# Two attentions of a two-block transformer kernel: scores as keys by tokens, less maxima found ahead of them

## The chip, the cores and the metric

The kernel runs on one core of one Trainium2 chip. It is one program for five engines: PE (TensorE, the matrix engine), DVE (VectorE), ACT (ScalarE), POOL (GpSimd) and SP (SyncE, which here only issues the transfers). The metric is the time of one launch in microseconds (us) on the device, lower is better; the figure compared is the median over runs. The trace comes from one more execution, which was profiled.

## The reference

Four sub-layers are added to a residual x of 256 tokens by 1024, all in float32: an NSA attention, a MoBA attention, a feed-forward, a mixer of two attentions (MLA and FoX), and a second feed-forward. The change is in the first two. With 256 tokens, NSA's selection takes every block and its window every earlier token, and MoBA has one block, so their scores are plain causal ones:

```
# NSA: three branches for each of 16 query heads (4 key heads), head size 64
s_cmp = q @ k_cmp.T * scale      # 15 compressed keys a head
s_slc = q @ ks.T * scale         # keys of branch 1, causal mask
s_win = q @ kw.T * scale         # keys of branch 2, causal mask
o = gc[..., 0:1] * o_cmp + gc[..., 1:2] * o_slc + gc[..., 2:3] * o_win
y = (o * silu(z)) @ w_out        # o_x = softmax(s_x) @ v_x
# MoBA: one causal branch
p = softmax(q @ k.T * scale + causal); y = ((p @ v) * silu(z)) @ w_out
# both: h = rms_norm(x) * (1 + scale) + shift;  x = x + gate * y, where
shift, scale, gate = split(silu(c) @ ada_w[i] + ada_b[i], 3)
```

## The kernel before

**Weights.** All weights are one list of units of 128 x 1024 floats (512 KB), fetched in order by SP into a ring of 7 buffers (`raw`, NRAW = 7). A buffer is fetched again when its unit has been used. For a projection, ACT rounds a unit to `w_hi` (`rounds`, L888, fp32r, up to 3 units ahead), DVE forms the rest `w_lo` (`rests`, L1313), and PE multiplies three times, hi by hi, hi by lo, lo by hi (`linear`): with tokens as output rows 512 columns at a time (L451, 12 matmuls a unit), or with tokens as columns 256 at a time (L460, 24 matmuls a unit). Matmuls on these rounded values are fp32r; the others (scores, values, transposes) are full fp32.

**Adaptive weights.** `ada_w` has 12 chunks of 512 columns, four units each. Chunks 0 to 3 are multiplied by cond and summed by DVE (`mac_chunk`, L1408). Of 4 to 11, ACT scales each half unit in place (`scale_chunk`) and POOL adds it to an accumulator (`sum_chunk`, L1952). PE then sums a chunk over partitions (`ada_columns`: L486, or L488 for the gate chunks).

**The order** is written out by hand for each engine, as a list of calls, and `hook(i, step)` puts pieces of other work between the items of an attention. For NSA it is: projection z0 (4 units), two matmul groups of compressed scores, then `attention` over 32 items, one for each head and branch; the four units of z1 sit in its first items; then out0 and out1 (8 units), the norm of the next sub-layer, and MoBA's projections. MoBA's attention has 16 items.

**An item of `attention`** goes through all engines. PE scores tokens by keys (L588, L589) in full fp32; DVE adds the causal mask and finds each row's maximum (L1484, L1486), and scales it (L1494); ACT takes exp with the maximum as bias and sums the row (L1007); DVE takes the reciprocal (L1491), multiplies by the gate (L1502) and divides (L1504, L1505); PE transposes the three 128 x 128 blocks (L475); ACT copies them back (`prob_t`); PE multiplies by the values (L610, L612; L609 for the compressed branch) into `o_acc`, 64 rows for each head. Scores are five items ahead of values. At every pair's end DVE multiplies by the gate z (L1470), ACT rounds (o_hi), DVE forms o_lo (L1509).

**Between sub-layers** (`norm_turns`, L504) x is multiplied by a diagonal matrix of the norm's factors while it is transposed; so PE waits for squares, mean, power (POOL) and the diagonal (L1336). After MoBA and after the mixer x is instead transposed as it is (`plain_turns`) and the factor is applied later.

## Time and profile before

| | |
|---|---|
| median of 3 runs | 1008.74 us (1004.24 to 1011.91) |
| the profiled execution | 1017.86 us, of which its span is 1016.0 |
| PE busy | 941.6 us, 93% of the span |
| DVE, ACT, POOL busy | 601.0, 515.5, 173.2 us |
| longest groups | L1313 DVE w_lo, 300.8 us; L888 ACT w_hi, 259.2 us |
| PE, full fp32 scores | L588 and L589: 33.9 and 43.7 us |
| PE, values | L609, L610, L612: 13.6, 47.3, 28.1 us (all attentions) |
| mean granted clock of PE | 0.952 |
| weights moved | 163.28 MB, at 161 GB/s |

A time here is the time an instruction stood in its engine; matmuls overlap, so the pace of PE is best read from the chain, which gives a run of matmuls with its length and their number. Each MATMUL of full fp32 shows as two instructions. "PEclk" is the granted clock in tenths, or as a share, of 2.4 GHz: 0.50 is 1.2 GHz.

### The profile page before, as it was taken

The numbers are of one execution on the slowest core, as the hardware profiler recorded it, in microseconds if no ns is written. First come the engines' busy times: TensorE is split into PE (matmuls) and PEld (weight loads), VectorE is DVE, ScalarE is ACT, GpSimd is POOL, SyncE is SP. The second block draws the span as 40 slices with busy tenths as digits, with TensorE's granted clock in tenths as the row PEclk, the third lists the DMA queues.
The fourth block names the chain that finished last, engine by engine and source line by source line (L and its number), as shares of the span: only waits on it lengthen the run. The fifth ranks groups of instructions, "written<-read, shape, count | busy, mean of one in ns | idle before, by whom it ended". The sixth has DMA issues, their size and how long they took to land.

```text
span 1016.0 us, 13211 instructions
## 1 busy us (share of the span) xinstructions
PE 941.6 (93%) x4823; PEld 763.2 (75%) x4823; DVE 601.0 (59%) x1192; ACT 515.5 (51%) x940; POOL 173.2 (17%) x190
## 2 busy tenths in 40 slices
PE   2689988998989988999999998999899899999997
PEld 2578976555568964788888887889788788888886
DVE  4873567766457577675555444659345765555542
ACT  2233556765434476564444443667555464444431
POOL 0015424652002651010000000426000200000000
PEclk9889999767699998999999999999999999999999
DMA  9855725444055453356555653645233555565651
GB/s 344 307 153 179 248 75 178 144 145 125 0 166 165 147 172 98 107 175 201 181 181 177 208 171 110 197 145 157 77 120 105 166 166 186 185 201 174 201 152 41
DMA packets 45391, 163.28 MB, mean 161 GB/s; under 512 B 5136, under 2 KB 5392, under 8 KB 45328
## 3 DMA queue, kind: packets, MB, share of 16 engines
q1 hardware_dynamic: 45328, 162.44, 50.0%
q8 instruction: 39, 0.64, 0.3%
q14 instruction: 24, 0.20, 0.1%
HBM read 161.37 MB, written 1.05 MB: 160 GB/s over the span
## 4 chain that ended last, share of the span: by engine, by line
PE 85%; DVE 8%; ACT 3%; issue 2%; DMA 1%; SPq 0%; POOL 0%; DVEq 0%; ACTq 0%
PE bank L451 55%; PE bank L460 11%; PE bank L475 5%; PE bank L610 3%; PE bank L589 2%; PE bank L588 2%; PE bank L504 2%; PE bank L547 1%; PE bank L612 1%; DVE w_lo L1313 1%; DVE ada_acc L1408 1%; PE bank L609 1%; DMA w_raw<-in_weights 1%; DVE stats L1494 1%; ACT soft L1007 1%
## 5 line engine op out<-in xcount | busy, mean ns | idle before, releaser
L888 ACT ACTIVATE w_hi<-w_raw 128x1024 fp32r<-128x1024 f32 (+2 forms) x249 | 259.2, 1047 | 203.0 <-PE bank L451 174.5
L1313 DVE TENSOR_TENSOR w_lo<-w_raw,w_hi 128x1024 fp32r<-128x1024 f32 (+2 forms) x249 | 300.8, 1224 | 101.3 <-ACT w_hi L888 101.3
L451 PE MATMUL bank<-w_hi,h_hi 128*128 128x512 f32 (+1 forms) x576 | 229.4, 398 | 15.6 <-DVE w_lo L1313 8.2
L451 PE MATMUL bank<-w_hi,h_lo 128*128 128x512 f32 (+1 forms) x576 | 225.4, 391 | 0.0
L451 PE MATMUL bank<-w_lo,h_hi 128*128 128x512 f32 (+1 forms) x576 | 224.9, 390 | 0.0
L451 PEld LDWEIGHTS bank<-w_hi,h_hi 128*128 128x128 f32 x576 | 109.5, 190 | 37.4 <-issue 16.5
L451 PEld LDWEIGHTS bank<-w_hi,h_lo 128*128 128x128 f32 x576 | 109.2, 190 | 22.9
L451 PEld LDWEIGHTS bank<-w_lo,h_hi 128*128 128x128 f32 x576 | 109.7, 190 | 20.9
L1952 POOL TENSOR_TENSOR ada_acc<-ada_acc,w_raw 128x512 f32<-128x512 f32 x56 | 73.4, 1311 | 84.0 <-ACT w_raw L892 79.4
L460 PE MATMUL bank<-h_hi,w_hi 128*128 128x256 f32 x264 | 77.9, 295 | 0.2 <-ACT tok_k L892 0.2
L460 PE MATMUL bank<-h_lo,w_hi 128*128 128x256 f32 x264 | 75.2, 285 | 0.0
L460 PE MATMUL bank<-h_hi,w_lo 128*128 128x256 f32 x264 | 75.1, 284 | 0.0
L451 PE MATMUL bank<-w_hi,a_hi 128*128 128x512 f32 x176 | 70.3, 400 | 0.0
L451 PE MATMUL bank<-w_hi,a_lo 128*128 128x512 f32 x176 | 69.3, 394 | 0.0
L451 PE MATMUL bank<-w_lo,a_hi 128*128 128x512 f32 x176 | 69.1, 392 | 0.0
L1007 ACT ACTIVATE soft<-soft,stats 128x128 f32<-128x128 f32 (+1 forms) x128 | 56.7, 445 | 12.6 <-DVE stats L1494 12.6
L892 ACT ACTIVATE prob_t<-bank 128x384 f32<-128x384 f32 x64 | 31.1, 487 | 62.9 <-PE bank L475 62.7
L1762 DVE SCALAR_TENSOR_TENSOR act<-bank,stats,act 128x256 f32<-128x256 f32 x44 | 21.1, 483 | 67.2 <-ACT act L1187 67.2
L460 PEld LDWEIGHTS bank<-h_hi,w_hi 128*128 128x128 f32 x264 | 51.1, 194 | 2.3 <-issue 1.8
L460 PEld LDWEIGHTS bank<-h_lo,w_hi 128*128 128x128 f32 x264 | 51.2, 194 | 0.2
L460 PEld LDWEIGHTS bank<-h_hi,w_lo 128*128 128x128 f32 x264 | 51.0, 193 | 0.0
L589 PE MATMUL bank<-k_t,q_t 64*128 64x256 f32 (+2 forms) x128 | 43.7, 431 | 0.0
(258 smaller groups left out, 1412.6 us busy)
## 6 DMA issues: line engine op xcount, KB each, us to landing
w_raw<-in_weights SPq DMA_DIRECT2D x298, 512.0 KB, 4.0
w_raw<-in_weights SPq DMA_DIRECT2D x4, 360.0 KB, 3.1
x<-in_x SPq DMA_DIRECT2D x1, 1024.0 KB, 7.0
gate_bias<-in_gate_bias SPq DMA_DIRECT2D x2, 512.0 KB, 9.4
out<-x SPq DMA_DIRECT2D x1, 1024.0 KB, 4.0
w_raw<-in_weights SPq DMA_DIRECT2D x3, 256.0 KB, 2.7
const<-in_constants SPq DMA_DIRECT2D x1, 413.5 KB, 7.7
cols<-in_columns SPq DMA_DIRECT2D x1, 208.5 KB, 2.5
```

The lines of the kernel that those rows point to most:

```text
L451: mm = e.matmul(pb[t][:, 0:n], xs[q], ws[p], start=(k + kk == 0 and i == 0), stop=(k + kk == kts - 1 and i == 2))
L460: mm = e.matmul(o, ws[p], xs[q], start=(k + kk == 0 and i == 0 and b % 2 == 0), stop=(k + kk == kts - 1 and i == 2 and (b % 2 == 1 or b == ...
L475: mm = e.transpose(bank[0:int(np.prod(src.shape[1:])), o:o + src.shape[0]], src, ident)
L504: mm = e.matmul(b[:, o:o + P], x[:, t, (2 * kp + kk) * P:(2 * kp + kk + 1) * P], diag[:, t, :], start=True, stop=True)
L589: e.matmul(bank[:, P:3 * P], it["q"](1), it["k"](S), start=True, stop=True).then_inc(*scored((s, i)))
L610: e.matmul(o, it["v"](0), p[:, 0:S], start=it["first"] and not it["cmp"], stop=False, skip_group_check=True)
L888: e.activation(w_hi[i % NSPLIT][:, 0:c], raw[v % NRAW][:, 0:c], ACT.Copy).then_inc(*rounded(v))
L892: return e.activation(out, src, ACT.Copy, **more)
L1007: e.activation(m[:, c0:c1], m[:, c0:c1], ACT.Exp, bias=ng[:, t:t + 1], scale=it["scale"], accum_out=su[:, t:t + 1]).then_inc(*exped((s, j, ...
L1313: e.tensor_tensor(w_lo[i % NSPLIT][:, 0:c], raw[v % NRAW][:, 0:c], w_hi[i % NSPLIT][:, 0:c].bitcast(F32), ALU.subtract).then_inc(*rested(v))
L1762: e.scalar_tensor_tensor(v, pairs[(p0 + n) % 2][tt][:, S:2 * S], norm_rs[i][:, tt:tt + 1], v, ALU.mult, ALU.mult).then_inc(*act_done((f, n ...
L1952: e.tensor_tensor(acc, acc, raw[u % NRAW][:, kk * 512:(kk + 1) * 512], ALU.add).then_inc(*ada_summed((c, k)))
```

## The change

1. **Scores.** `q_places` and `k_places` on ACT and the new `q_rests` and `k_rests` on DVE write q as hi and lo stacked on 128 partitions of `qs`, and k as `kh` (hi, twice) and `kl` (lo, and zeros). One fp32r matmul with kh then gives hi*hi + lo*hi, one with kl gives hi*lo. `pair_attention` replaces `attention` for NSA and MoBA: 8 slots of two items for NSA, 4 slots for MoBA; an item is two heads of one key head. `turned_scores` writes keys by tokens, adds the mask by a matmul, and takes the row's maximum off by matmuls of `minus_r` with the maximum `mx` broadcast. ACT takes exp straight from PSUM into `soft_t`, which PE uses as it lies (no transpose, no copy). `tokv` has ones beside the values, so the 65th column of a values matmul is the row sum. DVE's `evict` divides, gates and adds the three branches; the pair is then transposed once (`otok`).
2. **Maxima ahead.** `maxima_scores` on PE fills a bank 24 times for NSA and 12 for MoBA with scores of the rounded values (tokens by keys, and the mask), and DVE takes the maximum of each (`maxima`). They stand between the units of z0 and z1, which are now both ahead of the attention.
3. **Compressed branch.** Its scores are fp32r with 64 columns for each head; its factor is applied in `evict`.
4. **Adaptive chunks.** `ON_VECTOR` adds chunks 7 and 9 to those summed by DVE. The order of the units follows. Three units of nsa_out0 and two of nsa_out1 stand inside NSA's loop, four inside MoBA's.
5. **Norm ahead of the mixer** as `plain_turns`; its factors go into the eviction of the latents, the fox squares, scales and values, and `gate_scales` on DVE.
6. **Transfers.** The gate's bias lands in `gate_row`; its second fetch waits for the last use of gate_row in NSA, with the units from moba_z0 on behind it on SP (before: for chunk 5, with those from moba_q0 on). The output goes out in four parts.

```diff
 UNIT = 1024
+ON_VECTOR = (0, 1, 2, 3, 7, 9)
...
+            def turned_scores(s, i, x, free):
...
+                w.wait_ge(*m_reduced.at(last_filling(s, hb)))
+                for j, o in enumerate((oa, ob)):
...
+                    for m, k in enumerate((kh, kl)):
+                        e.matmul(o, k[:, g, br, j * P:(j + 1) * P], qs[:, ha:hb + 1:2, j * P:S], start=m == 0, stop=False,
+                    e.matmul(o[:, :, 0:P], mask_r[:, :], bcast(unit_r[:, :].unsqueeze(1), [P, 2, P]), start=False,
...
+                            mm = e.matmul(o[:, a, (t - j) * P:(t - j + 1) * P],
+                                          bcast(mx[:, t, h, it["mx"]:it["mx"] + 1], [P, P]), minus_r[:, :], start=False,
...
+                for i in range(n + 3):
+                    if i < n:
+                        turned_scores(s, i, 0, [[exped.at((s, i - 1, 0, 0))], [exped.at((s, i - 1, 1, 1))]] if i else
+                    if 0 < i <= n:
+                        values(i - 1, 1)
+                    if i < n:
+                        turned_scores(s, i, 1, [[exped.at((s, i - 1, 1, 0))] if i else bank_free[0],
...
+                    hook(i)
+                    if i < n:
+                        values(i, 0)
...
+                    if x == 0:
+                        for at in [o_evicted.at((s, i - 1))] if i else bank_free[1]:
...
+            def nsa_hook(i):
+                if i == 1:
+                    ada_columns(5, banks[0], pc_done.at(1))
+                if i in (4, 6, 8):
+                    next(outs[0])
+                if i in (9, 10):
+                    next(outs[1])
...
-                            if c in (1, 3):
-                                w.wait_ge(*ada_turned.at(c - 1))
+                            if c not in (0, 2):
+                                w.wait_ge(*ada_turned.at(c - 1 if c < 4 else c - 2))
...
+                if step_ == 1 and i < 8:
+                    mac_chunk(7 + i // 4 * 2, i % 4)
...
-            norm_turns(3, [a_rested.at((1, 8)), a_rested.at((1, 9)), a_rested.at((1, 10))])
...
-            w.wait_ge(*gate_row_done.at(5))
-            e.dma_start(gate_bias[:, :], gate_bias_d[1:2, :].to_broadcast([P, D])).then_inc(*bias1_in())
-            for u in range(of["moba_q0"][0], len(units)):
+            w.wait_ge(*y_gated.at(("nsa", 1, 1)))
+            e.dma_start(gate_row[:, :], gate_bias_d[1:2, :].to_broadcast([P, D])).then_inc(*bias1_in())
+            for u in range(of["moba_z0"][0], len(units)):
```

On PE, in the middle of NSA's attention, two items of the kernel before (the second branch of one head, then the first branch of the next, with its compressed values, L609):

```order
L588 MATMUL bank<-k_t,q_t 128x128
L589 MATMUL bank<-k_t,q_t 128x256
L475 MATMUL bank<-const,soft 128x128 x3
L610 MATMUL bank<-prob_t,tokv 64x256
L612 MATMUL bank<-prob_t,tokv 64x128
L588 MATMUL bank<-k_t,q_t 128x128
L589 MATMUL bank<-k_t,q_t 128x256
L475 MATMUL bank<-const,soft 128x128 x3
L609 MATMUL bank<-zs,vc 64x256
```

and of the changed kernel there, one item's scores and the values of the item before (L646 to L652 are `turned_scores`, L672 to L677 `values`; the last four rows stand for one of the item's two heads):

```order
L646 MATMUL bank<-qs,kh 128x512
L646 MATMUL bank<-qs,kl 128x512
L648 MATMUL bank<-unit_r,mask_r 128x2x128
L652 MATMUL bank<-minus_r,mx 128x128 x4
L646 MATMUL bank<-qs,kh 128x256
L646 MATMUL bank<-qs,kl 128x256
L648 MATMUL bank<-unit_r,mask_r 128x256
L652 MATMUL bank<-minus_r,mx 128x128 x2
L672 MATMUL bank<-tokv,soft_t 128x65
L673 MATMUL bank<-tokv,soft_t 128x65
L674 MATMUL bank<-tokv,soft_t 128x65
L677 MATMUL bank<-vc,zs 128x64 x2
```

The transposes are gone, the values have 65 columns in place of 256, and six matmuls of 128 columns for each item are new.

On DVE, an item of NSA's attention in the kernel before (ISA is the fused mask and maximum):

```order
L1484 ISA soft,stats<-bank,const 128x128
L1484 ISA stats 128x1
L1486 ISA soft,stats<-bank,const 128x256
L1486 ISA stats 128x1
L1491 RECIPROCAL stats<-stats 128x2
L1494 TENSOR_SCALAR stats<-stats 128x2
L1502 TENSOR_TENSOR stats<-stats,gates 128x2
L1504 TENSOR_SCALAR soft<-soft,stats 128x128
L1505 TENSOR_SCALAR soft<-soft,stats 128x256
```

and of the changed kernel DVE's work beside one unit of z1 (`maxima`, then `compressed_shift`, then the rest of a weight unit, then maxima again):

```order
L1671 TENSOR_REDUCE mx<-bank 128x4
L1671 TENSOR_REDUCE mx<-bank 128x2 x2
L1930 TENSOR_TENSOR scr<-bank,const 128x256 x2
L1930 TENSOR_TENSOR scr<-bank,scr 128x256 x2
L1936 TENSOR_REDUCE stats<-scr 128x16
L1938 TENSOR_SCALAR stats<-stats 128x16
L1940 TENSOR_TENSOR scr<-scr,stats 128x512
L1518 TENSOR_TENSOR w_lo<-w_raw,w_hi 128x1024
L1671 TENSOR_REDUCE mx<-bank 128x4
```

and DVE's work in one slot of the changed attention (`evict`, then a quarter of chunk 7 or 9):

```order
L1684 RECIPROCAL factors<-bank 128x2x2 x2
L1687 TENSOR_TENSOR factors<-factors,gates 128x2x2 x2
L1693 TENSOR_TENSOR parts_of_o<-bank,factors 128x384 x2
L1698 TENSOR_REDUCE tokq<-parts_of_o 128x2x64 x2
L1618 SCALAR_TENSOR_TENSOR ada_acc<-w_raw,cond,ada_acc 128x512 x2
```

The nine rows of each of 32 items have become six groups in each of 8 slots, and the maxima stand ahead, beside the units of z0 and z1.

## Rows read from the trace of the kernel before

**Rows 1.** The page: the granted clock of PE in the span's 40 slices.

```profile
PEclk9889999767699998999999999999999999999999
```

**Rows 2.** Windows: us, PE, PEld, DVE, ACT, POOL busy; clock, DMA share, GB/s.

```profile
124.60:299.30 174.70, 160.91 (x756) 112.11 (x755) 111.93 (x357) 100.11 (x248) 54.59 (x42) 0.81 0.40 124
...
150.00:180.00 30.00, 23.82 (x148) 17.71 (x148) 24.23 (x77) 18.33 (x50) 15.58 (x13) 1.00 0.54 176
...
240.00:270.00 30.00, 29.71 (x87) 17.55 (x88) 13.39 (x78) 10.32 (x37) 0.00 (x0) 0.50 0.15 52
...
353.70:437.40 83.70, 74.60 (x393) 53.68 (x393) 59.94 (x172) 53.99 (x133) 18.77 (x14) 0.96 0.39 124
375.00:390.00 15.00, 8.76 (x42) 4.98 (x42) 14.26 (x39) 12.54 (x31) 8.12 (x7) 0.97 0.46 134
395.00:410.00 15.00, 14.96 (x73) 8.33 (x72) 10.96 (x58) 10.69 (x40) 0.00 (x0) 0.96 0.00 0
624.80:633.40 8.60, 5.42 (x33) 5.45 (x34) 3.17 (x9) 3.29 (x9) 1.26 (x3) 0.80 0.01 2
```

**Rows 3.** Timeline of PE in NSA's attention: start, us, what.

```profile
211.93 1.12 PE L610 MATMUL bank<-prob_t,tokv 128*64 128x256 f32 x2
212.84 0.63 PE L612 MATMUL bank<-prob_t,tokv 128*64 128x128 f32 x2
...
272.24 0.59 PE L610 MATMUL bank<-prob_t,tokv 128*64 128x256 f32 x2
272.67 0.38 PE L612 MATMUL bank<-prob_t,tokv 128*64 128x128 f32 x2
```

**Rows 4.** The chain: start us, us, what, number of instructions.

```profile
82.18 7.09 PE bank L547 x64
...
98.17 0.87 PE bank L475 x8
...
124.58 8.63 PE bank L460 x72
...
276.67 22.61 PE bank L451 x96
...
347.94 8.63 PE bank L460 x72
...
431.86 8.34 PE bank L451 x36
...
627.98 5.43 PE bank L504 x32
...
951.97 58.81 PE bank L451 x252
```

**Rows 5.** Groups of DVE by form: count, busy us, mean ns, idle before.

```profile
L1313 DVE TENSOR_TENSOR w_lo<-w_raw,w_hi 128x1024 fp32r<-128x1024 f32 x242 | 295.2, 1236 | 89.6 <-ACT w_hi L888 89.6
...
L1408 DVE SCALAR_TENSOR_TENSOR ada_acc<-w_raw,cond,ada_acc 128x512 f32<-128x512 f32 x28 | 21.0, 752 | 6.7 <-DMA w_raw<-in_weights 5.2
...
L1375 DVE TENSOR_REDUCE stats<-squares 128x8 f32<-128x512 f32 x18 | 12.0, 684 | 14.4 <-ACT squares L924 12.4 <-ACT squares L938 2.0
...
L1470 DVE SCALAR_TENSOR_TENSOR gated<-bank,zs 128x256 f32<-128x256 f32 x16 | 6.7, 420 | 20.3 <-PE bank L612 20.3
...
L1491 DVE RECIPROCAL stats<-stats 128x2 f32<-128x2 f32 x64 | 10.4, 162 | 18.6 <-ACT soft L1007 18.6
```

**Rows 6.** The same of ACT.

```profile
L1187 ACT ACTIVATE act<-bank,stats 128x256 f32<-128x256 f32 x44 | 20.7, 476 | 22.5 <-PE bank L451 22.5
...
L892 ACT ACTIVATE a_hi<-bank 128x512 fp32r<-128x512 f32 x22 | 13.2, 598 | 38.1 <-PE bank L475 38.1
...
L892 ACT ACTIVATE w_raw<-w_raw,cond 128x512 f32<-128x512 f32 x56 | 37.5, 713 | 0.0
```

**Rows 7.** The page, part 6: transfers, KB, us to landing.

```profile
out<-x SPq DMA_DIRECT2D x1, 1024.0 KB, 4.0
...
w_raw<-in_weights SPq DMA_DIRECT2D x3, 256.0 KB, 2.7
```

More of the change, by code:

```diff
@@ L678, in nsa_hook @@
[L678 to L686 removed]
+                if j == 0:
+                    q_turns("nsa_q1", 0, banks[6], vc_done.at(3))
@@ L1969, in gpsimd @@
             head_ropes("nsa_q1")
-            for c in range(4, 10):
+            for c in (4, 5, 6, 8):
                 for j in range(4):
```

861 lines of the change are left out of this document (563 added, 298 removed).

## The prediction

> **What bounds the kernel now.** I read first the page's clock line and the windows, to see which stretches can give anything; then the chain, for the pace of PE by kind of matmul; then the timeline of an attention item; last the groups of DVE and ACT. PE stands in work nearly all the time, and in the feed-forwards, which the change leaves alone, the chain is one run of matmuls. What is not at PE's best pace lies in three places.
>
> NSA, from z0's first matmul at 124.58 to the end of nsa_out at 276.67 + 22.61 = 299.28 us, takes 174.7 us [rows 2, 4]. The granted clock averages 0.81 there: it is 1.00 while z1's matmuls stand between the items (150 to 180) and 0.50 for 30 us on end once they are gone (240 to 270), with PE "busy" 29.7 of the 30 us [rows 1, 2]. At 1.2 GHz a 256-column fp32 pair takes 0.91 us to the next start (211.93 to 212.84), at 2.4 GHz 0.43 (272.24 to 272.67) [rows 3]. MoBA, from the first unit of z1 (347.94 plus two units of 2.88 = 353.7) to the end of moba_out (431.86 plus two units of 2.78 = 437.4), takes 83.7 us; from 375 to 390 DVE is busy 14.3 of 15 us and PE 8.8, so there DVE's chain for each item bounds it [rows 2, 4]. And 8.6 us lie between the first feed-forward's last matmul and the mixer's first [rows 2], 5.43 of them the multiplying transposes [rows 4].
>
> **Prices on PE, all at 2.4 GHz.** An fp32r matmul of 512 columns 22.61/96 = 0.236 us, of 256 columns 8.63/72 = 0.120; a transpose 0.87/8 = 0.109; an instruction of full fp32 with 60 columns 7.09/64 = 0.111, so a matmul of 64 or 65 columns 0.22 (two instructions); fp32 with 512 columns twice the 0.43 of rows 3, 0.85 [rows 3, 4]. No row shows fp32r with 128 columns. From below, every row that loads fresh weights stands at 0.109 or more however few its columns; from above, a 128-column fp32 instruction takes 5.43/32 = 0.170, and even 0.236 would be a price of 512 columns. I take 0.11, since 256 columns take 0.120; there are 144 such matmuls in the slots of both sub-layers (12 slots of 12) and 16 in MoBA's fillings, so 0.17 adds 9.6 us and 0.236 adds 20.
>
> The Trainium skill (TensorE: Matmul & The Clock Gate, "Back-to-back issue gap") gives 134 cycles, 56 ns, for 128 columns; the same page's "LDWEIGHTS" gives P/1.2, 107 ns for 128 weight columns. By the first the 144 matmuls would cost 7.8 us less than in my sum; the trace's 0.109 and 0.111 rows agree with the second.
>
> **NSA, step by step.** PE's work from z0 to the end of nsa_out:
> - z0, z1: 8 units of 2.88 = 23.0. nsa_out: 96 x 0.236 = 22.6.
> - Fillings: one of each three is 0.236 + 2 x 0.12, two are 0.236 + 0.12; 1.19 each three, 8 times: 9.5.
> - Compressed scores 32 x 0.11 = 3.5; 32 transposes (q, compressed, outputs) 3.5; two gate chunks 1.7; four other chunks, 32 instructions of 0.11, 3.5.
> - Scores: an item 2 x 0.236 + 4 x 0.12 + 6 x 0.11 = 1.61; 16 items: 25.8.
> - Values: a slot 12 matmuls of 0.22 and 4 for the compressed branch, 3.55; 8 slots: 28.4.
>
> That is 121.5 us. The waits I walked through by DVE's and ACT's order. DVE's prices: w_lo 1.24, a maximum over 512 columns 0.68 (a reduce of the same size), a `mac` 0.75, 256 columns from PSUM 0.42, small ones 0.16 [rows 5]; q_rests and k_rests and a z product 0.69, by 512 columns at the rate of the 0.68 row.
> - z0: PE would need 17 us for units, fillings and transposes; DVE has 4 x 1.24 + 12 x 0.68 + 6 x 0.69 = 17.3. Filling 11 needs maximum 9, behind q_rests: a wait of 1.6.
> - z1: fillings use two banks only. Behind `compressed_shift` (4 x 0.42 + 0.68 + 0.16 + 1.24 = 3.8) and a w_lo, the maximum that frees filling 17's bank comes 6.3 us after the compressed scores, PE's other work is 3.6: 2.6. Again at filling 20: 1.4. The last maxima: 1.6.
> - The first values wait for the compressed transposes' copy, behind four exps: 0.7. At slot 1 DVE stands in `mac_chunk` on chunk 5's sum, which PE gives only in that slot's hook; then two macs and the eviction (2 x 0.16, 2 x 0.16, 2 x 0.55, steps between, 1.75) follow: 3.0.
> - Each later slot: the values of slot i wait for the eviction of i-1, 1.75 after its last values, PE's scores between take 1.61: 0.15. In slots 3, 5, 7 DVE also has gated, o_lo, two macs and a w_lo, 6 us against 5.1 of PE: 0.7 more each. With 0.9 for all slots' 0.15, 3.
>
> Together 13. ACT: a slot has two exps of 512 (0.60) and of 256 (0.48), two scalings of 0.71, half a w_hi: 4.1 of 7 us [rows 6], no bound. POOL adds 4 chunks, not 6. So NSA takes 134.5 us: **-40.2**. If the clock stays up, that is; the scores' matmuls and z1's are of the kind beside which it read 1.00.
>
> **MoBA.** z1 11.5, twelve transposes 1.3, fillings 4 x (0.236 + 4 x 0.11 + 2 x 0.36) = 5.6, slots 4 x (3.2 + 2.66) = 23.5, gate chunks 1.7, output transposes 1.7, moba_out 22.6, x's transposes 0.9: 68.9. Waits: q and k roundings on ACT and rests on DVE come together (12 copies and 6 of 0.69 behind z1's first unit), 1.7; the last maxima, 2; z_half and four scalings ahead of slot 1's exp on ACT, 0.5; 0.5 else. 73.6 against 83.7: **-10.1**.
>
> **Norm ahead of the mixer.** 16 transposes x 0.109 = 1.75, one more small matmul 0.4, 1 for roundings of the second half: 3.1 in place of 8.6: **-5.5**. If that half's roundings are late, the third unit of mix_lat waits and 2 of it are gone. The 8 `gate_scales` (0.69 each on DVE) lie under the mixer's PE work; uncovered they would cost 5.5. **Output:** a last part of 256 KB, 2.7 in place of 4.0 us [rows 7]: **-1.3**. The bias transfer holds back SP only from moba_z0 on, 12 units behind nsa_out with a ring of 7, so nothing; if it did hold, a fetch is one unit's time, under 3 us. The start has three more copies on ACT and memsets on POOL: nothing, at most 2, while the first transfers land.
>
> **Sum:** -57.1. Against the profiled execution's 1017.86 us that gives 960.8. The median of the runs before is 1008.74, 0.9% below that execution. In the same ratio the median after is 952; if the 9 us were only how long the clock stood low, they are gone anyway and it is 961. I take **956**.
>
> **The rivals.**
> *A, DVE becomes the bound in NSA.* For: a shift, a w_lo and the maxima are in one queue, `values` waits for an eviction each slot, and the small-looking steps of an item before already held PE at 8.8 of 15 us. Against: DVE's work in a slot is 5 us against 6.7. If each eviction takes 1.5 us longer (8 slots, 12 us) and z0 and z1 lose 8 more: 976.
> *B, narrow fp32r matmuls are dear.* At 0.236, 20 us more, of which the eviction waits give 2 back: 974.
> *C, the clock stays low through all slots.* For: the slots are more than half full fp32 instructions and 0.50 has been held for 30 us by such work; from 375 to 390 PE had waits and the clock fell after. Against: matmuls of 512 and 256 columns in every slot, and 395 to 410 stood at 0.96 without a projection beside [rows 2]. By the ratio of rows 3 a slot of 6.8 us becomes 12.4 or more: 8 x 5.5 + 4 x 5 = 64, and the five nsa_out and four moba_out units between, 9 x 2.8 = 25 if also low. With 64 to 89: 1020 to 1045. It decides from 57 us on, so when all slots are at 1.2 GHz; half of them give 990. The Trainium skill (TensorE: Matmul & The Clock Gate, "HAM oscillation") has the rate fall when the engine idles; by that rule this change, which takes waits out, would keep it up, and C would be no case; the 0.50 held with 29.7 of 30 us busy disagrees with it, so C keeps a chance [rows 2].
> *D, more is gained:* narrow matmuls at half my price and no evictions waited for: 16 us less, 940.
>
> **Chances.** The forecast 0.56 (945 to 970 by itself); A 0.20; B 0.07; C 0.07, half of it partial; D 0.10. The range, 936 to 985, leaves out C and the tails. A measurement tells about 1% from no change: faster by over 1% 0.93, within 1% 0.04, slower 0.03.
>
> **What would show it.** Right: PEclk near 1.0 from 125 to 260; nsa_out's last matmul near 259 us; slots of 6.9 us; L451 after the first feed-forward with no gap above 1 us. Wrong: PE waiting for maxima or evictions by more than 20 us in sum; MATMULs of `mx` spaced over 0.12; 0.5 in the clock line; POOL or DMA as the releaser anywhere in the slots.

## The result and the profile after

The changed kernel takes 1000.44 us in the median of nine executions, the kernel before 1016.14 in the median of nine (the three shown above are among them). The forecast was 956, with a range to 985. The executions of the changed kernel are of two kinds: seven from 999.66 to 1001.57 us, with a mean granted clock of 0.954 to 0.956, and two at 984.71 and 984.80, with 0.972. The ratio of the medians is 0.985; that of the faster kind to the kernel before is 0.972, with an interval from 0.964 to 0.979. The profiled execution took 1001.31 us, of which its span is 999.3, so it is of the usual kind, and every trace reading of the changed kernel below is of that kind.

The page of the changed kernel (span, engine, clock by slices, transfer):

```profile
span 999.3 us, 13019 instructions
...
PE 928.9 (93%) x5021; PEld 798.9 (80%) x5021; DVE 589.4 (59%) x933; ACT 475.6 (48%) x740; POOL 158.5 (16%) x178
...
PEclk9879898957989999999999999999999999999999
...
out<-x SPq DMA_DIRECT2D x4, 256.0 KB, 3.3
```

The clock line reads 5 and 7 in its ninth and tenth slices (200 to 250 us), where [rows 1] had 6 and 7. The chain of work of the changed kernel (start, us, what, number of instructions) gives the ends of the stages:

```profile
113.13 5.46 PE bank L491 x24
...
155.05 1.72 PE bank L599 x16
...
164.06 3.25 PE bank L599 x16
167.32 4.21 PE bank L491 x24
...
273.73 5.46 PE bank L482 x12
...
282.92 15.69 PE bank L482 x60
...
347.27 8.63 PE bank L491 x72
...
422.26 8.32 PE bank L482 x36
...
770.13 11.47 PE bank L491 x96
...
937.27 58.81 PE bank L482 x252
```

z0's first product stands at 131.15 us in the timeline, against 124.58 before; nsa_out ends at 282.92 + 15.69 = 298.61 us, against 299.28 before [rows 4]. MoBA runs from 347.27 plus two units of 2.88 = 353.0 to 422.26 plus two of 2.77 = 427.8. Windows of the changed kernel (us, busy time of PE, PEld, DVE, ACT, POOL, the clock, DMA):

```profile
110.00:113.00 3.00, 0.08 (x1) 0.00 (x0) 1.33 (x4) 1.45 (x3) 2.92 (x5) 0.84 0.88 280
113.00:116.00 3.00, 2.87 (x13) 2.90 (x14) 1.25 (x1) 0.00 (x0) 2.77 (x6) 0.50 1.00 330
...
119.00:122.00 3.00, 3.00 (x16) 2.53 (x16) 2.66 (x4) 1.76 (x3) 0.00 (x0) 1.00 0.22 37
...
200.00:205.00 5.00, 5.00 (x26) 5.00 (x24) 0.55 (x1) 0.98 (x2) 0.00 (x0) 0.50 0.37 105
...
230.00:235.00 5.00, 5.00 (x23) 4.81 (x23) 2.02 (x7) 0.14 (x1) 0.00 (x0) 0.50 0.82 289
...
240.00:245.00 5.00, 5.00 (x44) 4.91 (x45) 2.43 (x4) 3.18 (x5) 1.27 (x1) 1.00 0.14 16
...
353.00:427.80 74.80, 71.63 (x470) 64.14 (x469) 45.90 (x70) 42.75 (x69) 18.72 (x14) 0.98 0.43 138
```

From 200 to 235 us, in the middle of the slots, PE is busy 5.00 of every 5 us and has half its clock; with the full clock it gets through 44 matmul instructions in 5 us, with half of it 23 to 26. What stands ahead of that stretch is in the timelines of VectorE and of TensorE in slot 1 (start, us, what, and in brackets the idle time before it and who ended it):

```profile
192.35 0.48 DVE L1615 TENSOR_SCALAR ada_acc<-w_raw,cond 128x512 f32<-128x512 f32 x1 [9.31 <-PE bank L519]
192.87 1.64 DVE L1618 SCALAR_TENSOR_TENSOR ada_acc<-w_raw,cond,ada_acc 128x512 f32<-128x512 f32 x1
194.43 0.24 DVE L1684 RECIPROCAL factors<-bank 128x4 f32<-128x4 f32 x2
194.71 1.02 DVE L1687 TENSOR_TENSOR factors<-factors,gates 128x4 f32<-128x4 f32 x2
195.76 1.02 DVE L1693 TENSOR_TENSOR parts_of_o<-bank,factors 128x384 f32<-128x384 f32 x2
...
196.84 0.44 PE L672 MATMUL bank<-tokv,soft_t 128*128 128x65 f32 x2 [4.60 <-DVE parts_of_o L1693]
```

This is the wait that the prediction walked to: VectorE stands idle 9.31 us in `mac_chunk(7, 0)` until TensorE turns chunk 5's sum, then does two sums and only then the eviction, and the values of slot 1 wait 4.60 us for it (3.0 were forecast). The other large waits of TensorE between 105 and 300 us, by the view of waits (waiter, releaser, us in total, times, longest):

```profile
PE bank L621 <- DVE mx L1671: 5.6, 5, 2.6
...
PE bank L482 <- issue: 4.4, 2, 3.8
PE bank L491 <- DVE tokq L1600: 3.0, 1, 3.0
```

The first, 5.6 us for the maxima, the forecast had, and somewhat larger (1.6, 2.6, 1.4, and 1.6 ahead of the scores, 7.2 in all). The other two it had not. They are the wait of 3.05 us ahead of nsa_gate at 113.13, and one of 3.81 us at 273.73 ahead of nsa_out's third unit.

### The profile page after: what moved, and what is told of

It is laid out like the page before. It is cut to its first block, busy times and chain, and to the rows that moved or that the text cites. A ratio compares the mean times of both kernels' runs of the same rounds, so it can differ in the third digit from the quotient of the medians.

```text
span 999.3 us, 13019 instructions
## 1 busy us (share of the span) xinstructions
PE 928.9 (93%) x5021; PEld 798.9 (80%) x5021; DVE 589.4 (59%) x933; ACT 475.6 (48%) x740; POOL 158.5 (16%) x178
## 4 chain that ended last, share of the span: by engine, by line
PE 84%; DVE 8%; ACT 4%; issue 2%; DMA 1%; POOL 1%; SPq 0%; DVEq 0%; ACTq 0%
PE bank L482 55%; PE bank L491 11%; PE bank L506 4%; DVE w_lo L1518 2%; PE bank L646 2%; PE bank L652 1%; DVE mx L1671 1%; DVE ada_acc L1618 1%; PE bank L535 1%; PE bank L674 1%; PE bank L672 1%; PE bank L673 1%; ACT w_hi L1036 1%; PE bank L729 1%; DMA w_raw<-in_weights 1%
## 5 line engine op out<-in xcount | busy, mean ns | idle before, releaser
L1518 DVE TENSOR_TENSOR w_lo<-w_raw,w_hi 128x1024 fp32r<-128x1024 f32 (+2 forms) x249 | 306.8, 1249 | 82.2 <-ACT w_hi L1036 81.7
L2281 POOL TENSOR_TENSOR ada_acc<-ada_acc,w_raw 128x512 f32<-128x512 f32 x42 | 61.0, 1454 | 139.9 <-ACT w_raw L1040 136.9
L482 PE MATMUL bank<-w_hi,qs 128*128 128x512 f32 x128 | 46.0, 432 | 5.4 <-issue 4.4
L1145 ACT ACTIVATE soft_t<-bank 128x512 f32<-128x512 f32 x24 | 14.3, 596 | 61.7 <-PE bank L652 61.7
L1618 DVE SCALAR_TENSOR_TENSOR ada_acc<-w_raw,cond,ada_acc 128x512 f32<-128x512 f32 x42 | 36.6, 871 | 8.0 <-DMA w_raw<-in_weights 6.3
```

Of the source, the lines that this page charges most:

```text
L482: mm = e.matmul(pb[t][:, 0:n], xs[q], ws[p], start=(k + kk == 0 and i == 0), stop=(k + kk == kts - 1 and i == 2))
L1145: e.activation(soft_t[x][:, 0:2 * S], banks[4 + x][:, :], ACT.Exp, scale=HD ** -0.5).then_inc(*exped((s, i, x, 0)))
L1518: e.tensor_tensor(w_lo[i % NSPLIT][:, 0:c], raw[v % NRAW][:, 0:c], w_hi[i % NSPLIT][:, 0:c].bitcast(F32), ALU.subtract).then_inc(*rested(v))
L1618: e.scalar_tensor_tensor(acc, src, cond[:, k:k + 1], acc, ALU.mult, ALU.add).then_inc(*ada_mac((c, k)))
L2281: e.tensor_tensor(acc, acc, raw[u % NRAW][:, kk * 512:(kk + 1) * 512], ALU.add).then_inc(*ada_summed((c, k)))
```

## The experiments

Each kernel is the changed kernel, or one of the kernels below, with the edit shown. Times are medians of four executions or six, each beside executions of the kernel before (medians 1014.77 to 1017.25). "The kernel with the later sums" is that of the first experiment.

### Does the wait in slot 1 let the clock fall?

**The sums one slot later.** VectorE's sums of chunks 7 and 9 come behind the eviction of the slot before:

```diff
@@ nsa_hook of VectorE
                 if step_ == 0 and i == 1:
                     z_products("nsa_z1", 1, 1, 0)
                     z_products("nsa_z1", 1, 1, 1)
+                if step_ == 0 and 0 < i < 9:
+                    mac_chunk(7 + (i - 1) // 4 * 2, (i - 1) % 4)
...
-                if step_ == 1 and i < 8:
-                    mac_chunk(7 + i // 4 * 2, i % 4)
```

> The changed kernel with VectorE's sums of chunks 7 and 9 one slot later, behind the eviction of the slot before and behind z1's products, so that no eviction stands behind a sum that waits for the chunk ahead. Theory C (the clock): in the changed kernel's trace TensorE waits 4.60 us at 196.84 for VectorE and its granted clock is 0.50 from 200 to 235, where a slot takes 13.5 us instead of 6.9; the wait is what lets the clock fall. Then here the wait is under 1.5 us, the clock stays near 1.00 through the slots, and the profiled execution ends 4.6 + about 18 us earlier, and 3 to 4 more at the end of the attention, where a rounding for VectorE no longer stands behind a sum: 972 to 980 us. Theory F (the fp32 products of the slots by themselves hold the clock low, whatever the waits are): the clock is 0.50 in the slots all the same and only the waits go: 990 to 996 us. Theory N (the wait moves elsewhere, since chunk 5's sum is late anyway): 997 to 1001 us.

Measured: 974.15 us (973.05 to 974.79), ratio 0.960 [0.958, 0.962]. This is what theory C expected, in the time and in the clock. The window of that kernel over the slots has no low clock left, and its chain has nsa_out's end at 256.17 + 15.57 = 271.74 us, 26.9 earlier than in the changed kernel:

```profile
195.00:240.00 45.00, 44.81 (x352) 42.65 (x351) 32.08 (x60) 19.88 (x37) 15.51 (x10) 1.00 0.51 154
```

```profile
256.17 15.57 PE bank L482 x60
```

**The wait kept, but filled.** 20 products that nobody reads, `mask_r` against `unit_r`, stand in it:

```diff
@@ nsa_hook of TensorE
                 if i == 1:
                     ada_columns(5, banks[0], pc_done.at(1))
+                    w.wait_ge(*z_done.at(("nsa_z1", 1)))
+                    for _ in range(20):
+                        e.matmul(banks[2][:, :].rearrange("p (g n) -> p g n", n=P), unit_r[:, :],
+                                 bcast(mask_r[:, :].unsqueeze(1), [P, 4, P]), start=True, stop=True, ...)
@@ nsa_hook of VectorE
                     compressed_factors(1)
-                if step_ == 0 and i == 1:
                     z_products("nsa_z1", 1, 1, 0)
                     z_products("nsa_z1", 1, 1, 1)
```

The second part moves VectorE's products with z1 ahead, into its idle time, so that the bank of the needless products is free.

> The changed kernel with 20 needless fp32r products of 512 columns (0.22 us each, together 4.4) in TensorE's wait of 4.60 us in slot 1, and z1's products ahead of VectorE's sum, into its idle time, so that the bank for them is free. The wait for VectorE stays as long; TensorE is only busy in it. Theory C (the idle time lets the clock fall): the clock stays near 1.00 in the slots, and the profiled execution takes 979 to 984 us though it does 4.4 us of work more. Theory F (the slots' own products hold it low): the clock is 0.50 from about 200 us on and the time is 999 to 1001 us. The two lie 15 us and more apart.

Measured: 984.26 us (983.07 to 984.85), at the upper edge of theory C's 979 to 984, and all four executions as fast as the two fast ones of the changed kernel. More work, 16.2 us less span (983.1 against 999.3). Timeline and windows of that kernel:

```profile
191.57 5.14 PE L819 MATMUL bank<-mask_r,unit_r 128*128 128x512 f32 x20
```

```profile
200.00:235.00 35.00, 34.32 (x275) 32.84 (x275) 24.97 (x48) 15.45 (x30) 9.17 (x6) 1.00 0.37 121
```

So 16.2 of the 26.9 us are the clock alone, and 4.6 are the wait in slot 1. Where the rest lies, the times of three traces tell (us):

| kernel | chunk 5's sum | last values end | nsa_out ends | the slots between | the end behind them |
|---|---|---|---|---|---|
| changed kernel | 191.17 | 269.92 | 298.61 | 78.8 | 28.7 |
| the wait filled | 191.06 | 251.72 | 281.44 | 60.7 | 29.7 |
| the later sums | 191.42 | 245.84 | 271.74 | 54.4 | 25.9 |

In the slots the clock is worth 18.1 us (78.8 against 60.7). The filled kernel gives some of that back: its last 60 products of nsa_out take 17.06 us against 15.69, and its end is 1.0 us longer. The later sums save 4.6 us of wait and 1.6 more in the slots, which was not divided. At the end they save 2.8: VectorE's `w_lo` of nsa_out's third unit stands behind its sums, TensorE waits 3.81 us for it at 273.73, and the unit takes 5.46 us at half the clock; with the later sums it is 2.13 and 4.58. The slots' own fp32 products do not bring the clock down: here they ran at 1.00 throughout. The Trainium skill (TensorE: Matmul & The Clock Gate, "HAM oscillation") has the rate fall when the engine idles; these two kernels agree.

**Who sums.** The same order as the first kernel, with chunks 7 and 9 scaled by ScalarE and summed by GpSimd (`ON_VECTOR = (0, 1, 2, 3)`, a second `scale_chunk` a slot, and GpSimd's sums in turn).

> The same as the run with the later sums, but chunks 7 and 9 are scaled by ScalarE and summed by GpSimd, as in the kernel before: that part of the change is undone alone. If it does not matter who sums, the time is that of the run with the later sums within 3 us: two GpSimd sums of 1.45 us for each of two units are 5.8 us in a slot of 6.9. If GpSimd then becomes late, the column sums of chunks 6 to 9 stand in TensorE's order and it waits for them: 5 to 15 us over that run. If VectorE's sums were what costs (each stretched from 0.75 to 1.6 us beside GpSimd's), it is 3 to 6 us under it.

Measured: 990.61 us (990.18 to 991.64), 16.5 over the kernel with the later sums, just beyond the 5 to 15 of the second case: GpSimd is late, and twice TensorE waits for it ahead of the column sums (5.52 us at 223.70, 4.18 at 268.00), each time with low clock behind. Timeline and window:

```profile
223.70 1.87 PE L517 MATMUL bank<-const,ada_acc 128*128 128x1 f32 x8 [5.52 <-POOL ada_acc L2281]
```

```profile
225.00:238.00 13.00, 13.00 (x58) 12.61 (x59) 2.60 (x10) 1.48 (x3) 0.00 (x0) 0.50 0.20 75
```

The change's choice of VectorE for the two chunks is thus worth 16.5 us, if they stand where they make no eviction wait.

**VectorE's load itself.** In the kernel with the later sums, only 32 of the 512 columns of chunks 7 and 9 are summed (`[:, 0:m]` with m = 32 for them); the rest of the two chunks is left out.

> The kernel with the later sums (974.15 us), but VectorE sums only 32 of the 512 columns of chunks 7 and 9, so that each of its 32 sums takes about 0.1 us instead of 0.75 (the rest of the two chunks is left out). It asks what VectorE's load still costs once no wait stands in its way. If VectorE is the bound of the attention's steps (it is busy 4.89 of 5 us at 205 to 210 and 9.50 of 10 at 240 to 250): up to 8 us less, 966 to 970. If it only has work, and TensorE is the bound: 0 to 2 us less, from the wait of 2.13 us at 247.97 for the rounding behind it: 972 to 974.

Measured: 971.80 us (970.88 to 974.73), 2.4 less by the medians, though the slowest of the four is no faster than with the sums whole. VectorE's work in the slots is hidden; rival A, that VectorE's load becomes the bound, is refuted for all but those 2 us.

### The start and the end of the stage

**The keys' placing behind nsa_q1's squares.** On ScalarE the eight copies of `k_places` go behind `head_squares("nsa_q1")`, on VectorE both `k_rests` behind `head_sums("nsa_q1")`.

> The changed kernel with the eight ScalarE copies that place the keys (0.70 us each) behind nsa_q1's squares instead of ahead of them, and VectorE's rests of the keys behind nsa_q1's sums. In the changed kernel nsa_gate's first product comes at 113.13 after a wait of 3.05 us, against 108.96 in the kernel before. If the placing ahead of the squares makes it late, it comes at about 110, everything behind is 3 us earlier, and the slots' clock is untouched: about 3 us under the changed kernel, 996 to 997 profiled. If the wait is for the queue of ScalarE as a whole, it only moves: 999 to 1000. A change of which clock the slots get would show as 15 us more or less in single executions.

Measured: 999.62 us (990.05 to 1005.00). The wait did not go, its releaser is the same operation, and it is longer, since on VectorE the scaling now stood behind the rests and two more roundings; and the four executions differ by 15 us, with mean clocks from 0.949 to 0.967, so a gain of 1 or 2 us could not be seen. The expectation was too simple. Timeline:

```profile
113.64 0.55 PE L491 MATMUL bank<-h_hi,w_hi 128*128 128x256 f32 x1 [4.74 <-DVE tokq L1599]
```

**Three orders.** The later sums; the keys as above, but with `head_scales("nsa_q1")` ahead of the second `k_rests`; nsa_out's rests a slot earlier and ahead of the last column sums:

```diff
@@ nsa_hook of VectorE
-                if step_ == 1 and i in (3, 5, 7):
+                if step_ == 1 and i in (2, 4, 6):
                     rests(of["nsa_out0"][i // 2 - 1], 0)
@@ cmp_w1_1 of VectorE
                 if j == 0:
-                    k_rests("nsa_kskw", "nsa_ks", 0, banks[4])
-                    k_rests("nsa_kskw", "nsa_kw", 1, banks[6])
                     head_sums("nsa_q1")
-                if j == 3:
+                    k_rests("nsa_kskw", "nsa_ks", 0, banks[4])
+                if j == 1:
                     head_scales("nsa_q1")
+                    k_rests("nsa_kskw", "nsa_kw", 1, banks[6])
```

> The kernel with the later sums, and two more orders changed: the keys' placing stands behind nsa_q1's squares on ScalarE and nsa_q1's scaling ahead of the second keys' rests on VectorE; and the rests of nsa_out's units come one step earlier, ahead of the last column sums. With the keys' placing alone TensorE still waited (4.74 us at 113.64, since the scaling stood behind the rests and two roundings), and its clock was 0.50 from 113 to about 117. If both the wait (3.05 us in the changed kernel) and the low clock behind it (nsa_gate and the first unit of nsa_vsvw: about 3 us) go: 5 to 6 us less, and 2 to 3 at the end of the attention: 965 to 968 us. If only the wait goes: 969 to 971. If it moves to another releaser: 973 to 975.

Measured: 968.46 us (967.47 to 969.92), just above the first case (965 to 968), but not for its reason: ahead of nsa_gate 2.42 us of wait are left, with another releaser, and the clock behind them is low again. z0 begins at 129.56 instead of 131.53, and NSA takes 135.9 us. Timeline and windows:

```profile
112.74 0.55 PE L491 MATMUL bank<-h_hi,w_hi 128*128 128x256 f32 x1 [2.42 <-ACT w_hi L1036]
```

```profile
129.50:265.40 135.90, 126.58 (x893) 116.07 (x892) 99.62 (x176) 64.26 (x105) 41.29 (x28) 0.97 0.48 155
```

**The first keys' copies in ScalarE's idle time** (`k_places` of `nsa_ks` ahead of the squares, of `nsa_kw` behind), six executions:

> The kernel with three orders changed (968.46 us), with the first keys' four copies placed ahead of nsa_q1's squares, into time in which ScalarE stood idle (7.55 us at 101.88), and only the second keys' four behind them. There the wait ahead of nsa_gate is 2.42 us for a rounding on ScalarE, and the clock behind it is at the low level again (0.83 over 110 to 120). If ScalarE's queue is what makes nsa_gate late: the wait goes, and with it the low clock: 963 to 966 us. If the wait only gets shorter and the clock still falls: 966 to 968. If it was the transfer of the weights: 968.

Measured: 967.94 us (967.04 to 971.82), ratio 0.955 [0.951, 0.958]: the same as the kernel with three orders within its spread, with a wait of 2.29 us for the same rounding. The keys' copies are no longer in the chain. What stands there is the order on ScalarE still: the rounding comes behind two activations (`hid`) that wait for TensorE's own products, which end at 110.13.

```profile
106.60 3.53 PE bank L578 x32
...
110.15 0.51 ACT hid L1233 x2
110.67 0.96 ACT w_hi L1036
111.62 0.79 issue
112.41 4.48 PE bank L491 x24
```

No transfer of weights stands in it. Whether the wait would go with the rounding ahead of `hid` was not tried. This is the fastest kernel of the study, level with the one of three orders and 32 us below the changed one.

**The output in one transfer**, on the kernel with the later sums, six executions:

> The kernel with the later sums (974.15 us), with the output stored by one transfer of 1024 KB at the end, as in the kernel before, instead of four of 256 KB: that part of the change is undone alone. By the durations from issue to landing (4.0 us for the one, 3.3 for each of the four, of which the last is what counts): 0.7 us more. By the prediction 1.3 more, 975.5. By the ends of the two traces 2.0 more, 976.2. If the four small transfers disturb each other: no change, 974.

Measured: 975.91 us (974.68 to 979.99), 1.8 more by the medians, which is within the spread of the executions; the ends of the traces decide. VectorE's last addition and the span, in that kernel and in the one with four transfers:

```profile
core 0 of [0], span 972.8 us
...
967.57 0.69 DVE L1664 SCALAR_TENSOR_TENSOR x<-bank,x 128x512 f32<-128x512 f32 x1 [0.71 <-PE bank L482]
```

```profile
core 0 of [0], span 972.3 us
...
969.13 0.69 DVE L1664 SCALAR_TENSOR_TENSOR x<-bank,x 128x512 f32<-128x512 f32 x1 [0.71 <-PE bank L482]
```

From the start of that addition to the end it is 5.2 us with one transfer and 3.2 with four: 2.0.

### Why does the clock stay low for 40 us?

Needless copies ahead of one exponential make ScalarE late and TensorE wait, in the kernel with the later sums:

```diff
@@ pair_attention of ScalarE
+                        for _ in range(13 if s == "nsa" and i == 4 and x == 0 else 0):
+                            w.wait_ge(*idled.now())
+                            copy(squares[:, 0, :], squares[:, 1, :]).then_inc(*idled())
                         e.activation(soft_t[x][:, 0:2 * S], banks[4 + x][:, :], ACT.Exp,
```

**In slot 4:**

> The kernel with the later sums (974.15 us), plus 13 needless ScalarE copies (0.6 us each) ahead of the exponentials of slot 4, of which about 3 us lie beside TensorE's work, so that TensorE stands idle for about 5 us in the middle of the slots. Nothing else is changed. If idle time lets the clock fall and the slots do not bring it back soon, as in the changed kernel (0.50 from 200 to 235): 5 us for the wait and 10 to 18 more, 989 to 997 us, and a granted clock of 0.50 in slots 5 to 7. If slot 1 of the changed kernel was special (chunk 5's sum, the fp32 turns just ahead of it): 979 to 980 us, and the clock stays at 1.00.

**Between the first two units of moba_q0,** a power and two additions of GpSimd for which TensorE waits:

> The kernel with the later sums (974.15 us), plus about 4.7 us of idle time on TensorE between the first and the second unit of moba_q0, a stretch of fp32r products of 512 columns (GpSimd does a needless power and two additions, and TensorE waits for them). In the changed kernel the wait of 3.05 us ahead of nsa_gate was followed by a granted clock of 0.50 for some 5 us only, then 1.00 again. If what follows the idle time decides how long the clock stays low: 4.7 us and 2 to 4 more, 981 to 983 us, against 10 to 18 more in the slots. If the idle time alone decides: the same 10 to 18 us more as in the slots, 989 to 997. If the clock does not fall here: 978 to 979.

**In slot 1,** 13 copies, then 9, then 18:

> The kernel with the later sums (974.15 us), plus the 13 needless ScalarE copies ahead of the exponentials of slot 1 instead of slot 4. In slot 4 they made a wait of 6.32 us at 218.00; the granted clock was 0.51 at 215 to 220 and 1.00 again from 225, while the first unit of nsa_out (12 products of 512 columns to a half, all fp32r) ran: 981.4 to 986.2 us in four executions. Behind slot 1 no such unit comes before slot 4. If it is the slots' own mix (fp32 products of 64, 65 and 128 columns) that keeps the clock at the low level, as in the changed kernel: low to slot 4, 6 us for the wait and 13 to 18 more, 993 to 999 us. If the low level ends by itself wherever it begins: 980 to 987, as with slot 4.

> The kernel with 13 needless copies in slot 1 (wait of 5.66 us at 196.58, clock back at 1.00 from about 201, 984.33 us), with 9 of them: a wait of about 3.2 us. It asks whether the length of the wait decides how long the clock stays low behind it: after 4.60 us at this place it was 40 us in the changed kernel, after 5.66 about 5. If the length decides in either direction, the four executions agree within 3 us, at 979 to 982 (clock low shortly or never) or at 992 and more (low for long, as after 4.60). If it is not the length: executions of one kernel differ by 5 us and more.

> The same with 18 copies: a wait of about 8.7 us. If a longer wait makes the low level longer: over 984.3 + 3 + 5 = 992 us. If the low level behind it stays about 5 us: 986 to 989. If the length decides nothing: executions differ by 5 us and more.

**The changed kernel's own wait, longer,** by four copies on VectorE ahead of the first eviction:

> The changed kernel, with four needless VectorE copies (together 1.5 to 2.5 us) ahead of the first eviction, so that TensorE's wait in slot 1 is about 6.5 instead of 4.60 us; its place and what follows it are the changed kernel's. If a wait of this length has the clock back after 5 us here too, as with ScalarE's copies: 984.7 + 2 = 986 to 988 us in every execution. If what stands around the wait (VectorE's late eviction, the slots in step with it) keeps the clock low: 1001 to 1004 in most. If neither decides, both kinds of execution, some 16 us apart, as in the changed kernel (1000.4 and 984.7).

**Dense products in slot 2 of the changed kernel,** 20 of them, some 12 us behind the wait:

> The changed kernel (1000.44 us in seven of nine executions or near it, 984.7 in two), its wait of 4.60 us in slot 1 untouched, plus 20 needless fp32r products of 512 columns in slot 2, right behind the fall of the clock: 4.4 us at the high level, 8.6 at the low. If a stretch of dense fp32r products brings the clock back where the slots' own do not: 1.00 from about 215 instead of 238, some 11 us won and 7 spent: 994 to 998 us. If the products do nothing for the clock: 1005 to 1009. If the clock hangs on something else than TensorE's products, the spread of the changed kernel comes back: some executions near 990, others near 1008.

**Dense products right behind the wait** of the changed kernel, 12 of them ahead of the first values of slot 1 (and VectorE's products with z1 moved ahead, as in the filled kernel):

```diff
@@ values of TensorE
+                    if s == "nsa" and (i, x) == (1, 0):
+                        w.wait_ge(*z_done.at(("nsa_z1", 1)))
+                        for _ in range(12):
+                            e.matmul(banks[2][:, :].rearrange("p (g n) -> p g n", n=P), unit_r[:, :],
+                                     bcast(mask_r[:, :].unsqueeze(1), [P, 4, P]), start=True, stop=True, ...)
                     for a, h in enumerate(it["heads"]):
```

> The changed kernel with its wait of 4.60 us in slot 1, and right behind that wait, ahead of the values' products of 65 columns, 12 needless fp32r products of 512 columns (2.8 us at the high level, 5.2 at the low); z1's products stand in VectorE's idle time, so that their bank is free. In the runs so far the clock was back within 5 to 7 us wherever products of 256 or 512 columns came first after the wait (nsa_gate, nsa_out's and moba_q0's units, the scores after 5.66 and 8.96 us), and stayed low for 15 to 40 us where the values' or the column sums' came first (the changed kernel, 4.60 and 6.60 us; GpSimd's late sum, 5.52). If what comes first decides: the clock is back by about 203, and the time is 984.7 plus 3 to 5, 987 to 990 us, in every execution. If it does not: 1003 to 1006 us in most.

What these runs and the ones above measured, by the wait of TensorE in the profiled execution, what it does first behind it, and when the windows read 1.00 again:

| kernel | median, lowest to highest | wait, at | first behind it | clock 1.00 again by |
|---|---|---|---|---|
| changed kernel | 1000.44, 984.71 to 1001.57 | 4.60, 196.84 | values, 65 columns | 239 |
| the same, longer wait | 1002.21, 992.53 to 1005.49 | 6.60, 197.89 | values | 239 |
| GpSimd's sums | 990.61, 990.18 to 991.64 | 5.52, 223.70 | column sums, values | 240 |
| 20 dense in slot 2 | 1000.83, 994.14 to 1006.92 | 4.59, 195.33 | values | 211, in their midst |
| 12 dense right behind | 988.92, 986.10 to 991.49 | 4.59, 196.38 | those, 512 columns | 202 |
| 9 copies, slot 1 | 986.75, 980.35 to 994.89 | 3.01, 190.69 | scores of 256 and 128, then chunk 5's sum, 512 | 195 |
| 13 copies, slot 1 | 984.33, 982.52 to 985.54 | 5.66, 196.58 | the same | 201 |
| 18 copies, slot 1 | 986.73, 985.71 to 987.71 | 8.96, 198.79 | the same | 204 |
| 13 copies, slot 4 | 983.65, 981.31 to 986.16 | 6.32, 218.00 | scores of 256 and 128, then a unit, 512 | 222 |
| in moba_q0 | 984.93, 980.61 to 987.86 | 4.89, 287.97 | unit, 512 columns | 293 |

Windows of three of them: the longer wait, 18 copies, and the dense products right behind.

```profile
198.00:237.00 39.00, 39.00 (x172) 37.84 (x172) 19.24 (x38) 9.52 (x17) 6.48 (x4) 0.50 0.24 85
```

```profile
199.00:202.00 3.00, 3.00 (x9) 1.97 (x10) 0.00 (x0) 1.82 (x4) 0.78 (x1) 0.50 0.00 0
203.00:240.00 37.00, 36.81 (x294) 35.29 (x294) 25.62 (x50) 15.98 (x30) 11.04 (x8) 1.00 0.43 134
```

```profile
196.00:201.00 5.00, 4.62 (x11) 3.67 (x12) 2.83 (x5) 0.00 (x0) 0.00 (x0) 0.50 0.69 233
202.00:220.00 18.00, 17.92 (x149) 17.36 (x149) 11.04 (x23) 8.26 (x16) 3.98 (x3) 1.00 0.18 59
```

Every wait of TensorE of 3 us and more in the traces of this study, from the start of nsa_gate on, is followed by the low clock: in the slots, ahead of nsa_gate, in moba_q0, ahead of the turns of x. Shorter ones are followed by it mostly, not always: 2.61 us at 163.12 in the changed kernel was, 2.82 us at 152.01 in the kernel before was not. The length of the wait does not set how long the clock stays low: 6.60 us of VectorE's are followed by 40 us, 8.96 of ScalarE's by 5. Nor does the place: slot 1 stands in both.

What goes with it in the table is what TensorE does first. Where products of 256 and 512 columns came first, the clock is back in 4 to 6 us; where the values' 65 columns or the column sums' single ones did, it takes 15 to 40 in the slots. In the two runs of 40 us it comes back 2 to 3 us into the first unit of nsa_out, of 512 columns (from 235.63 and 237.11), and in the run with 20 dense products, which begin at 208.19, some 3 us into them. The run with 12 wide products right behind the wait tests this: all four of its executions came out at 986 to 991 with 12 products more to do, and in its trace the clock is back before those 12 end. The moving of VectorE's products with z1 that goes with its edit was not run alone, so it is not excluded as a helper. The expectations that the slots' mix would keep the clock low wherever it fell (slots 1 and 4) both failed: there wide products came first. Of the others, the longer wait came out by its second case (three of four at 1001.73 to 1005.49), 18 copies by the one that expects some 5 us, 9 copies and the dense products in slot 2 by the spread (14.5 and 12.8 us between executions), and moba_q0 nearest its first, at 984.93 for 981 to 983.

Width is not the whole account. Ahead of the turns of x (L535), in the changed kernel, a wait of 3.93 us at 302.52 is followed by 32 instructions of full fp32 with 128 columns, and the clock is back by 308. Behind GpSimd's second wait, at 268.00, with column sums first and a unit of nsa_out next, it took 9 us. In the kernel before, a wait of 2.73 us ahead of full fp32 products of 256 columns is followed by 0.50 until about 270.

Nor is it a law. Two of nine executions of the changed kernel have a mean clock of 0.972 without any edit; whether it never fell there or came back early no trace shows. With dense products 12 us later two executions of four took 994.14 and 996.51, against 1005.14 and 1006.92. With 9 copies two took 992.68 and 994.89 us, and in the profiled one, at 980.83, the clock fell once more, from about 221 to 231, with TensorE busy all the while; what stands ahead of that are 16 column sums of one column, from 217.65 to 219.77:

```profile
220.00:226.00 6.00, 6.00 (x34) 5.86 (x34) 0.04 (x1) 1.95 (x4) 1.28 (x1) 0.61 0.49 167
```

What decides in the single execution stays open.

## Why the prediction was wrong, step by step

Against the profiled execution the sum gave 960.8 us and 1001.31 came. The 40.5 us between them:

| step | forecast | measured | missed by |
|---|---|---|---|
| start of z0 | no change | 131.15 instead of 124.58 | 6.6 |
| NSA, z0 to nsa_out's end | 134.5 | 298.61 - 131.15 = 167.5 | 33.0 |
| MoBA | 73.6 | 427.8 - 353.0 = 74.8 | 1.2 |
| norm ahead of the mixer | -5.5 | -5.1 | 0.4 |
| output | -1.3 | -2.0 | -0.7 |

**NSA is where it failed, in one sentence:** "If the clock stays up, that is; the scores' matmuls and z1's are of the kind beside which it read 1.00." The prediction asked which products the clock likes. It should have asked what each wait in its own list does to the clock: it had written down a wait of 3.0 us in slot 1 and priced it at 3.0. It cost 4.6 and 16.2 behind it (the filled wait against the changed kernel). The trace of before had the hint. The 30 us of half clock that the prediction puts down under rival C to the slots' kind of work, and to z1's matmuls being gone [rows 2], begin behind a wait of TensorE (timeline of PE):

```profile
240.29 1.11 PE L609 MATMUL bank<-zs,vc 128*64 128x256 f32 x2 [2.73 <-DVE gated L1470]
```

So that row is no evidence against a clock that falls when TensorE idles, which is how the prediction used it. The 5.43 us of the turns of x ahead of the mixer, from which it took 0.170 us as a bound at the high level, stand behind a wait too, of 3.21 us, and the clock over that stretch is 0.80 [rows 2, 4].

**The work and the waits of NSA were nearly right.** With the three orders changed NSA takes 135.9 us at a clock of 0.97, without slot 1's wait; the sum without it is 131.5. (The sum's own waits add to 13.9 us, not 13, so it should have read 135.4 with that wait and 132.4 without.) The narrow fp32r product stands at 0.10 us (four of L652 from 186.36 to 186.75) against 0.11 taken, so rival B falls, and the waits for maxima are 5.6 us in five pieces. Of the 33.0 us missed, 18.1 are the clock in the slots behind the wait (16.2 for the kernel as a whole), 1.6 the wait there (4.6 for 3.0), 1.6 the rest of the slots, 2.8 the end of the attention, 0.9 the addition. The other 8 are in the kernel with the later sums too, whose 140.2 us must be set against 132.4. About 3 of them are low clock behind the longest wait for a maximum, 2.6 us in z1: the compressed scores behind it take 3.25 us where those before it took 1.72, and the unit 4.21 instead of 2.88. Another 4.3 went with the three orders. The rest was not divided further.

**The start failed as a step:** "three more copies on ACT and memsets on POOL: nothing, at most 2". The placing of the keys is eight copies of 0.70 us and four rests, all ahead of nsa_q1's squares, in the one place where TensorE has nothing else left: nsa_gate waits 3.05 us for the scaling, and then takes 5.46 us for what takes 2.88 at the high level [rows 4], because the clock is low from 113 to about 118. Again a wait and its clock. Of the 6.6 us, 3.05 are this wait, 2.4 the low clock in nsa_gate (5.46 against 3.06 in the kernel before), and 1.1 lie ahead of it (TensorE's products there end at 110.08, in the kernel before at 108.96). In the changed kernel the chain runs through the eight copies; with them moved, 2.3 to 2.4 us of wait stayed for other reasons and z0 began 2 us earlier, so the copies alone are not the whole of it. The prediction costed some copies, not the queue that they stand in.

**The end of the attention was not walked.** VectorE's and ScalarE's roundings for nsa_out's units were costed in the slots, but not who waits for them: 3.81 us at 273.73, and a unit at half the clock. With the later sums 2.8 us of this went.

**MoBA, the norm and the output were right** within 1.2 us. In MoBA TensorE has no wait as long as in NSA and the clock is 0.98. The norm: by the chain the changed kernel is 437.4 - 427.8 = 9.6 us ahead at moba_out's end and 784.82 - 770.13 = 14.7 at the first long run of 256-column products of the mixer, so 5.1 come between. The output was mis-sized: 2.0 by the traces, 1.8 by the medians, for 1.3; the four transfers take 3.3 us each from issue to landing, but only the last counts and it is issued at once.

The chain of the kernel before at that place:

```profile
784.82 11.47 PE bank L460 x96
```

**The rivals.** B fell, and so did D, that more is gained. A fell as it was meant, as VectorE's load; but it is VectorE's order, with an eviction behind sums, that made the wait. C, with its "half of them give 990", was the nearest in time and had the right effect with the wrong cause: it made the slots' products to blame, and gave it 0.07, half of that partial. The range ended at 985, just under it. Taking 956 from 960.8, for the median of three executions, made the miss larger: over nine executions the median of the kernel before is 1016.14, not 1008.74.

## What to carry to other kernels

In these traces a wait of TensorE of 3 us or more cost itself and the low clock behind it: 1 to 4 us more where the clock was back in about 5 (profiled executions of the copies in slots 1 and 4 and of moba_q0, against the later sums), 16 where it stayed low for 40. So list the waits of a forecast and price each with its clock; in a kernel, put nothing ahead of an eviction that can wait for TensorE itself (here two lines moved by one slot gave 26 us), and where a wait can't be taken out, look at what stands first behind it (here 12 wide products there gave 11 us). Work moved to another engine is to be priced by the queue that it stands in: the eight copies cost 0.7 us each on ScalarE, and TensorE waited 3.05 us behind the chain that they are in, with 2.4 us of low clock after it.

## What the runs showed of the hardware

Waits of TensorE in the same slot 1 are followed by 4 us of half clock in one kernel and by 40 us in another (3.01 us at 190.69 with 9 copies, 4.60 at 196.84 in the changed kernel), and executions of one unchanged kernel differ by 16 us (984.71 and 1001.57) with mean clocks of 0.972 and 0.954. Work added in an idle place made the kernel 16 us faster.

VectorE and GpSimd slow each other: VectorE's second sum at 192.87 takes 1.64 us, and the mean over the changed kernel is 0.87 where it was 0.75 before [rows 5]; it has GpSimd's sum of 1.52 us beside it, from 192.44, and that sum takes 1.28 us where VectorE is idle (at 186.62). The Trainium skill (SBUF — State Buffer, "SBUF: two separate sides") says that a VectorE operation with two inputs in SBUF and a GpSimd operation share one pair of ports and that the later one is held up; this row agrees. With the sums cut to 32 columns the gain was 2.4 us, so here it stays off the path.
